# Key products moved from GpSimd to VectorE, key pages asked for earlier, and the block softmax begun earlier and cut into more pieces

## The reference

```
gate = einsum('bhqd,bhnd->bhqn', q, kmean);  _, sel = top_k(gate, 3)
s = einsum('bhqd,bhqkjd->bhqkj', q, ks) * scale;  p = softmax(where(mask, s, -inf))
out = einsum('bhqkj,bhqkjd->bhqd', p, vs)
```

## The kernel before

| what | before | after |
|---|---|---|
| last key reduced on DVE, awaited by PE | block 131, awaited at 134 | block 129, awaited at 128 |
| maximum (`max_dve` 3): DVE, awaited by PE | +5, +7 | +8, +7 |
| turned maximum (`max_tr`): PE, awaited by DVE | +7, +8 | +7, +11 |
| diagonal (`max_dve` 5): DVE, awaited by PE | +8, +9 | +11, +9 |
| `max_mm`: PE, awaited by DVE | +9, +10 | +9, +13 |
| sums (`p_sum`): DVE, awaited by PE | +12, +13 | +15, +13 |
| `p_mm`: PE, awaited by DVE | +13, +14 | +13, +17 |
| own row (`p_done`): DVE, awaited by PE | +14, +15 | +18, +17 |

## Time and profile before

### The profile page before, as it was taken

The page is one execution under the profiler, slowest core; times in us unless marked ns, Lnnn a source line. Parts: engine busy times, 40 slices in busy tenths (PEclk is TensorE's granted clock), DMA queues, the critical chain, the costliest instruction groups (busy, mean ns, idle before and its releaser), DMA issues.

```text
span 1858.6 us, 35476 instructions
## 1 busy us (share of the span) xinstructions
PE 1819.9 (98%) x14803; PEld 1747.5 (94%) x14803; DVE 1212.7 (65%) x1682; ACT 864.0 (46%) x1447; POOL 209.3 (11%) x124
## 2 busy tenths in 40 slices
PE   8999998999999999999999999999999999999997
PEld 8999997998898989888999899999999999999997
DVE  6479898799897656653764556666666666444444
ACT  5444555554444334542444465554545554433442
POOL 2155543543000000000000000000000000000000
PEclk9999999999999999999999999999999999999999
DMA  8599876977668797877565277777777776655552
GB/s 246 163 312 305 299 246 197 304 250 249 183 197 287 250 293 258 278 258 250 172 202 185 91 244 231 224 233 224 224 230 224 231 226 208 212 182 175 164 181 88
DMA packets 387039, 417.03 MB, mean 224 GB/s; under 512 B 10560, under 2 KB 364768, under 8 KB 385792
## 3 DMA queue, kind: packets, MB, share of 16 engines
q10 hardware_dynamic: 284336, 285.35, 48.4%
q1 hardware_dynamic: 102336, 128.75, 21.2%
q0 software_dynamic: 208, 0.67, 0.2%
HBM read 396.37 MB, written 18.63 MB: 223 GB/s over the span
## 4 chain that ended last, share of the span: by engine, by line
PE 86%; DVE 9%; issue 1%; ACT 1%; DMA 1%; ACTq 0%; POOL 0%; SPq 0%; DVEq 0%; POOLq 0%
PE gemm L1657 27%; PE gemm L1658 26%; PE gemm L1659 26%; DVE w_lo L1129 4%; PE side L1922 2%; PE side L1619 1%; DVE sc_flat L1325 1%; DVE conv_out L1123 1%; ACT w_hi L739 1%; PE side L1620 1%; DMA xtok<-in_x_prompt 0%; PE side L1943 0%; DMA kv<-in_cache_k 0%; DVE u L1123 0%; PE side L1869 0%
## 5 line engine op out<-in xcount | busy, mean ns | idle before, releaser
L1129 DVE TENSOR_TENSOR w_lo<-raw,w_hi 128x1024 fp32r<-128x1024 f32 (+1 forms) x562 | 732.5, 1315 | 453.2 <-ACT w_hi L739 452.3
L1657 PE MATMUL gemm<-x_hi,w_hi 128*128 128x264 f32 x3344 | 968.2, 290 | 22.3 <-DVE w_lo L1129 21.0
L1659 PE MATMUL gemm<-x_hi,w_lo 128*128 128x264 f32 x3344 | 950.5, 284 | 0.0
L1658 PE MATMUL gemm<-x_lo,w_hi 128*128 128x264 f32 x3344 | 950.3, 284 | 0.0
L739 ACT ACTIVATE w_hi<-raw 128x1024 fp32r<-128x1024 f32 (+1 forms) x562 | 579.5, 1044 | 403.9 <-PE gemm L1659 403.2
L1657 PEld LDWEIGHTS gemm<-x_hi,w_hi 128*128 128x128 f32 x3344 | 633.3, 189 | 50.9 <-issue 26.1
L1658 PEld LDWEIGHTS gemm<-x_lo,w_hi 128*128 128x128 f32 x3344 | 634.0, 190 | 1.2 <-issue 0.5
L1659 PEld LDWEIGHTS gemm<-x_hi,w_lo 128*128 128x128 f32 x3344 | 630.4, 189 | 0.0
L1658 PE MATMUL gemm<-g_lo,w_hi 128*128 128x264 f32 x704 | 200.4, 285 | 0.0
L1657 PE MATMUL gemm<-g_hi,w_hi 128*128 128x264 f32 x704 | 200.1, 284 | 0.0
L1659 PE MATMUL gemm<-g_hi,w_lo 128*128 128x264 f32 x704 | 199.5, 283 | 0.0
(11 more groups left out here) (312 smaller groups left out, 1372.7 us busy)
## 6 DMA issues: line engine op xcount, KB each, us to landing
raw<-in_w_in ACTq DMA_DIRECT2D x99, 1024.0 KB, 7.3
raw<-in_w_gate ACTq DMA_DIRECT2D x44, 1024.0 KB, 6.3
raw<-in_w_up ACTq DMA_DIRECT2D x44, 1024.0 KB, 5.8
raw<-in_w_down ACTq DMA_DIRECT2D x40, 1024.0 KB, 5.4
kv<-in_cache_k SPq DMA_DIRECT2D x64, 512.0 KB, 5.8
kv<-in_cache_v SPq DMA_DIRECT2D x64, 512.0 KB, 5.3
st<-in_state_ssm SPq DMA_DIRECT2D x64, 256.0 KB, 4.0
raw<-in_w_ssm_out ACTq DMA_DIRECT2D x16, 1024.0 KB, 6.9
```

The costliest lines, as they stand in the source:

```text
L1129: v.tensor_tensor(w_lo[:, s, 0:blk.kts, cols], raw[:, s, 0:blk.kts, cols], w_hi[:, b % RING, 0:blk.kts].bitcast(fp32), ALU.subtract).then_ ...
L1657: mm(out, w_hi[:, b % RING, k], pr.hi[:, x], start=(x == 0), stop=False)
L1658: mm(out, w_hi[:, b % RING, k], pr.lo[:, x], start=False, stop=False)
L1659: ins = mm(out, w_lo[:, s, k, cols], pr.hi[:, x], start=False, stop=(x == pr.kt - 1))
```

## The change

Key products: POOL's `keys` is gone, DVE multiplies and then reduces a page in one step, at K_AT[m]. K_AT is now `30 + int(1.58*m)`, blocks 30 to 129. SP asks for a page at K_AT[m]-8. The softmax is based on SEL = 128, and DVE's part is spread over steps SEL+3, 5, 6, 7, 8, 11, 13, 15, 17, 18 and 21; PE's second block sum is at SEL+2 and its own-row product at SEL+17; ACT's exponential is at SEL+14.

```
-K_PACE = 1.64
+K_PACE = 1.58
-        SEL = 134
+        SEL = 128
-        K_AT = [26 + int(K_PACE * m) for m in range(NB * NPG)]
+        K_AT = [30 + int(K_PACE * m) for m in range(NB * NPG)]
@@ sync, key_loads
-                    if b != max(K_AT[m] - 6, ROWS[0] + 5):
+                    if b != max(K_AT[m] - 8, ROWS[0] + 5):
@@ gpsimd
-            def keys(b):
-                for m in range(NB * NPG):
-                    if b != K_AT[m]:
-                        continue
-                    n = m // NPG
-                    if m % NPG == 0:
-                        gp.wait_ge(qb_in, 16 * (n + 1))
-                    gp.wait_ge(kv_in[m % 4], 16 * (m // 4 + 1))
-                    gp.tensor_tensor(out=page_slot(m), in0=page_slot(m), in1=qb[:, n % 2, :], op=ALU.mult)\
-                        .then_inc(k_mul, 1)
@@ scalar, softmax
-                if b == SEL + 11:
+                if b == SEL + 14:
@@ vector, keys
-                    if b == K_AT[m] + 2:
+                    if b == K_AT[m]:
-                        dve.wait_ge(k_mul, m + 1)
+                        if g == 0:
+                            dve.wait_ge(qb_in, 16 * (n + 1))
+                        dve.wait_ge(kv_in[m % 4], 16 * (m // 4 + 1))
+                        then(dve, mul(page_slot(m), page_slot(m), qb[:, n % 2, :]), k_mul, m + 1)
@@ vector, softmax
-                if b in (SEL + 2, SEL + 5):
-                    n = (b - SEL - 2) // 3
+                if b in (SEL + 3, SEL + 5):
+                    n = (b - SEL - 3) // 2
...
+                if b == SEL + 6:
                     drained(v.tensor_scalar(rest, m_w[:, 3, :], -1.0, 1.0, ALU.mult, ALU.add))
...
+                if b == SEL + 7:
                     for n in range(NBLK):
...
+                if b == SEL + 8:
                     v.tensor_reduce(out=m_w[:, 5, :], in_=scp.rearrange("p g x -> p x g"), axis=AX.X, op=ALU.max)\
                         .then_inc(max_dve, 1)
-                if b == SEL + 8:
+                if b == SEL + 11:
...
-                if b == SEL + 10:
+                if b == SEL + 13:
...
-                if b == SEL + 12:
+                if b == SEL + 15:
...
-                if b == SEL + 14:
+                if b == SEL + 17:
...
+                if b == SEL + 18:
...
-                if b == SEL + 17:
+                if b == SEL + 21:
@@ tensor, softmax
-                if b in (SEL, SEL + 3):
-                    n = (b - SEL) // 3
+                if b in (SEL, SEL + 2):
+                    n = (b - SEL) // 2
...
-                if b == SEL + 15:
+                if b == SEL + 17:
```

More of the change, by code:

```diff
@@ L732, in _ @@
             for b in range(END):
-                keys(b)
                 ends(b)
```

## The result

The changed kernel takes 1862.51 us, the median of 20 runs, against 1857.45 of 20 runs of the kernel before. The ratio is 1.0021, its 95% interval 1.0013 to 1.0029: 3.9 us slower by the ratio, 2.4 to 5.4 by its interval (the two medians are 5.1 apart). The forecast was +2.3 us.

A forecast was written before the change was run, and what follows sets the result against it. PE bounds the kernel, with 17.2 us of waits for DVE to win. Blocks 60 to 100 give -3, pages 0, blocks 110 to 150 +5.3: +2.3 on the 1857.2 median, rounded to 1860 us, range 1848 to 1872.

The forecast's parts named there:

- D and E: Blocks 110 to 130 and 130 to 150 together: PE loses 14.7 us instead of 9.4, so +5.3.
- What bounds the kernel: Whole run: PE, busy 98%; its waits for DVE's `w_lo` between 200 and 560, 17.2 us, are all there is to win.
- The product, 1.25 us: Each of the 64 key products costs DVE 1.25 us, 80 in all; bounds 1.1 and 1.35 each.
- What DVE gets back: DVE instructions slowed while POOL multiplies recover their whole excess, 19.8 us on `w_lo` in blocks 60 to 100.
- Stretch B: Blocks 60 to 100: PE loses 5 us instead of 7.85 as bursts get better, -3 (bounds -8 and +2).
- DVE pays in full: Rival: the excess is not POOL's, nothing comes back in blocks 110 to 130; 1873 us, chance 0.05.
- Stretch A: Blocks 26 to 40: no loss to win and DVE's load hardly moves, 0.
- Stretch D and the way into the softmax: From block 110: PE stands until DVE ends the maximum at 499, losing 13.2 us instead of 5.2.
- The wait at 137: PE issues `y_mm` and waits for DVE's step 139, where `u` comes first: some 1 us.
- What E wins: Blocks 130 to 150: the 7.6 us burst of selecting in one step goes, with PE's loss of 3.75 around it.
- the backlog: Rival: DVE's lead at block 110 is gone and its backlog becomes idle PE; 1868 us, to 1873; chance 0.18.
- All bursts were POOL's: Rival: nearly every late `w_lo` in blocks 60 to 100 and 110 to 130 is POOL's disturbance; 1848 us, chance 0.17.

The follow-up runs named there:

- run 4: The changed kernel with the products left out, raw pages reduced as they landed (scores not the reference's): 1842.86 us, ratio 0.9922 to the kernel before.
- run 7: Changed keys with the old softmax (SEL = 134), products on DVE up to page 50 and on POOL from page 51: 1861.61 us, ratio 1.0018.
- run 1: The changed kernel with the 64 products on POOL again, two blocks before the same DVE steps: 1860.61 us, ratio 1.0011.
- run 2: The changed kernel with PE turning the maximum one step later, at SEL+8 = 136: 1861.27 us, ratio 1.0020.
- run 12: Pace 1.42, softmax from SEL = 123 with its meetings apart, products on POOL two blocks ahead: 1852.88 us, ratio 0.9973.
- run 11: The changed kernel with key pace 1.42 and the softmax from SEL = 123, its meetings further apart, products on DVE: 1857.36 us, ratio 0.9990.
- run 3: The changed keys with the softmax of before (SEL = 134, selection in one step): 1858.90 us, ratio 1.0003.
- runs 9 to 12: Four kernels with key pace 1.42, sharing a chip: old softmax 1860.25 us, changed softmax 1860.53, meetings apart 1857.36, that with POOL's products 1852.88.

## Why the prediction was right, and where its sizes were off

**The total**: the sign was right and the size short, +2.3 for 3.9 by the ratio, just outside its 2.4 to 5.4. That the two traces differ by +2.1 is luck, as the parts below show: D and E were put 2.2 too low, and that is made up by A and B, which came out better, and by 1.3 us that are none of the change's.

**What bounds the kernel**: right. The change moved PE's waits for DVE and the half clock behind them. Run 4, with no product anywhere, is some 15 us below the kernel before, which is near the 17.2 that the waits were said to be worth.

**The product, 1.25 us**: right, 1.21 to 1.22 and the reduction 1.25 after its start. **What DVE gets back**: right, 74.6 us in all, so DVE's total rose by 3.3. `w_lo` in stretch B took 49.3 us for 69.85. The undisturbed `xdts` and `u` at the same place of step 79 show it best, beside the earlier trace rows:

```profile
278.53 0.77 DVE L1110 SCALAR_TENSOR_TENSOR u<-conv_th,conv_out 128x264 f32<-128x264 f32 x2
279.41 0.19 DVE L1107 TENSOR_TENSOR xdts<-u,scal 128x32 f32<-128x32 f32 x1
```

The Trainium skill's rule on the shared pair (page "SBUF — State Buffer", section "Who interferes with whom"), that a DVE instruction with two SBUF inputs contends with a GpSimd instruction that reads SBUF, agrees with all three cases here: POOL's products with slow `w_lo`, none of either, and both engines at once in run 7 (3.30 and 3.40 us). The rival that DVE pays in full is refuted by the 74.6 us that came back, and by run 1.

**Stretch B, -3**: measured -3.5. **Stretch A, 0**: -0.6.

**Stretch D and the way into the softmax**: the mechanism was right, the size short. From PE's start on block 110 to its going on after step 135 I had 92.4 + 13.2 = 105.6; it was 498.98 - 389.21 = 109.8. Two terms of the sum carry the difference. DVE's lead at block 110 was taken over from before, 5.4 us; it was 2.5 (389.21 - 386.72), which makes 2.9:

```profile
386.72 1.22 DVE L1116 TENSOR_TENSOR w_lo<-raw,w_hi 128x1024 fp32r<-128x1024 f32 x1
```

DVE's own products in the blocks before are the lesser part of that: run 1, with POOL's products at the same new places, has a lead of 3.6 there, and run 4, without products, 7.2. The prediction had a lead used up among its bounds, not in its sum. DVE's way from there to the maximum's end took 112.1 for 111: 1.1. The stand at 135 itself was read from the timeline as a floor of 4.2 whatever the load, and is 3.8 (3.85 in the timeline, not the "4 us or more" forecast) with DVE full, with POOL's products, and with no products. The wait at 137 was put at 1 and is 0.4, with 1.6 at 141 that I had among the 0.5 for the rest.

**What E wins**: -2.7 from block 136 to 150 by my sums (4.2 lost before, 1.5 after), -4.7 measured (55.9 for 60.5). Most of the rest is the half clock, which the sum left out on both sides: 6.8 us of it before near block 140, 3.4 after, a difference of some 1.5 us in PE's time. D and E together: +5.3 forecast, +7.5 measured. With -0.6, -3.5 and -1.3 from blocks 200 to 240 that makes the span's +2.1; that stretch has nothing of the change in it; its clock was 0.98 on average in the kernel before and 1.00 in the changed one in blocks 200 to 220, with the stretch of half clock at 798.4 in the former alone, behind waits that both have.

**The rivals**: the backlog in part, as PE's wait at 128 is for one; its condition, no lead at 110, was half met. Run 2 shows that shortening one wait gives little where DVE is behind. All bursts were POOL's: no, for with POOL's products gone B still loses 4.3 us where that rival had 1, and D 10.0 where it had 2.

What stays open is why POOL's products win with the faster pace (run 12 against run 11) and lose nothing in blocks 60 to 100. The change's own softmax with the meetings apart and pace 1.58 was not run, nor was POOL with the old softmax and the new places.

## What to carry to other kernels

When engines walk through the same steps at a lead, place a meeting so that each side is asked for it as many steps late as the other may be behind: in run 11, with PE a step or more after DVE's and DVE three or more after PE's, no stand at a meeting was left. Before moving one, lay the other groups' meetings over it. If PE waits in front of its next block for an answer that needs PE's own last products and three steps on two other engines, it stands even when DVE has time: 3.85 us here, with the products on either engine and with none.

A stand of a few microseconds on PE often has a second price, a stretch of half clock worth 1.5 us. And a product moved from POOL to DVE is neither the relief of the one nor the full load of the other: here DVE got back 74.6 us of 77.9, and the time was level within 2 us at one pace and 4.5 us better on POOL at another.

## What the runs showed of the hardware that was not expected

PE's clock falls to 0.50 around stands that are short beside the run: behind 3.85 us at 498.9, and at 407.73 in block 114, after PE had stood 2.07 us in block 112 and 2.24 in block 113 for `w_lo`. In run 2 it fell from 500.42 on behind a stand of only 1.00 us and, one matmul later, 0.80. Without products (run 4), PE stood 1.2 us at block 113 and the clock stayed full.

The same stand does not always bring it. The 2.52 us of the changed kernel in block 124 did not. The 2.07 and 2.23 us of blocks 112 and 113 brought 3.4 us of half clock in the changed kernel and none in run 3. The 2.40 us in block 147, nearly the only wait behind block 120 in runs 11 and 12, brought it in run 11 alone. The 3.01 us before block 140 brought 6.8 us in the kernel before and 3.4 in run 3. So a difference of 1.5 us between two traces can be one such stretch and nothing of the edit, and part of the scatter between executions goes with it: of the kernel before, beside runs 9 to 12, the fastest of 28 took 1853.06 us at a mean clock of 0.993 and the slowest 1869.37 at 0.988.

Leaving 78 us of DVE work out of a kernel whose DVE is 65% busy gave 18 to 20 us.

DVE's own product is held as long as `w_lo` is: 3.30 us for 1.22 while POOL multiplied. POOL's product took 2.40, no more than its median before (2.42).
